# Two wide chunks in the second up unit of each group, and the moved block read a unit sooner

## The reference

```python
h = rmsnorm(x, norm_mlp[l])
x = x + jnp.square(jax.nn.relu(h @ w_up[l])) @ w_down[l]
```

## Time and profile before

| | |
|---|---|
| median of 3 runs | 2680.71 us |
| span of the profiled execution | 2676.6 us |
| TensorE products busy | 2663.6 us (100%) |
| DVE busy | 2049.1 us (77%) |
| ACT busy | 1447.3 us (54%) |
| wide chunks (L1336) | 166 |
| plain chunks of 1024 (L1315) | 762 |

### The profile page before, as it was taken

The page is one execution under the profiler, slowest core; times in us unless marked ns, Lnnn a source line. Parts: engine busy times, 40 slices in busy tenths (PEclk is TensorE's granted clock), DMA queues, the critical chain, the costliest instruction groups (busy, mean ns, idle before and its releaser), DMA issues.

```text
span 2676.6 us, 37287 instructions
## 1 busy us (share of the span) xinstructions
PE 2663.6 (100%) x13592; PEld 2234.4 (83%) x13592; DVE 2049.1 (77%) x3019; ACT 1447.3 (54%) x1863; POOL 128.0 (5%) x220
## 2 busy tenths in 40 slices
PE   9999999999999999999999999999999999999998
PEld 7788778888888888888887887788888888888887
DVE  5665568977798897987756655689678988989875
ACT  5545555545665555655455455555456556556554
POOL 0100000000100100100010000000001001000000
PEclk9999999999999999999999999999999999999999
DMA  7875545676775766766687655466677767667574
GB/s 259 234 238 165 181 158 183 227 243 234 233 232 192 242 220 205 241 208 225 233 231 230 215 169 178 157 201 229 227 258 236 227 201 241 211 218 231 191 247 151
DMA packets 179960, 575.55 MB, mean 215 GB/s; under 512 B 23016, under 2 KB 43028, under 8 KB 179664
## 3 DMA queue, kind: packets, MB, share of 16 engines
q1 hardware_dynamic: 166256, 536.94, 61.4%
q0 software_dynamic: 13008, 35.98, 5.1%
q10 hardware_dynamic: 528, 0.37, 0.1%
HBM read 535.15 MB, written 38.04 MB: 214 GB/s over the span
## 4 chain that ended last, share of the span: by engine, by line
PE 98%; DVE 1%; DMA 0%; issue 0%; ACT 0%; POOLq 0%; POOL 0%; ACTq 0%
PE acc L530 25%; PE acc L532 25%; PE acc L531 25%; PE att L500 2%; PE att L498 2%; PE att L499 2%; PE acc L498 2%; PE acc L500 2%; PE acc L499 2%; PE acc L548 1%; PE acc L547 1%; PE acc L546 1%; PE turn L499 1%; PE turn L500 1%; PE turn L498 1%; PE att L625 0%
## 5 line engine op out<-in xcount | busy, mean ns | idle before, releaser
L1315 DVE TENSOR_TENSOR w_lo<-raw,w_hi 128x1024 fp32r<-128x1024 f32 (+1 forms) x778 | 935.2, 1212 | 422.8 <-ACT w_hi L890 420.1
L890 ACT ACTIVATE w_hi<-raw 128x1024 fp32r<-128x1024 f32 (+1 forms) x778 | 813.7, 1052 | 683.9 <-PE acc L532 512.6
L530 PE MATMUL acc<-w_hi,h_hl 128*128 128x512 f32 x1848 | 736.7, 399 | 1.0 <-DVE w_lo L1315 0.9
L532 PE MATMUL acc<-w_hi,h_hl 128*128 128x512 f32 x1848 | 729.0, 394 | 0.0
L531 PE MATMUL acc<-w_lo,h_hl 128*128 128x512 f32 x1848 | 728.5, 394 | 0.0
L530 PEld LDWEIGHTS acc<-w_hi,h_hl 128*128 128x128 f32 x1848 | 347.9, 188 | 84.1 <-issue 5.5
L532 PEld LDWEIGHTS acc<-w_hi,h_hl 128*128 128x128 f32 x1848 | 347.8, 188 | 81.5
L531 PEld LDWEIGHTS acc<-w_lo,h_hl 128*128 128x128 f32 x1848 | 348.3, 188 | 75.9
L1336 DVE TENSOR_TENSOR w_lo<-raw,w_hi 128x1792 fp32r<-128x1792 f32 x166 | 335.5, 2021 | 41.2 <-ACT w_hi L899 40.2
L530 PE MATMUL acc<-w_hi,o_hl 128*128 128x512 f32 x912 | 361.0, 396 | 0.0
L531 PE MATMUL acc<-w_lo,o_hl 128*128 128x512 f32 x912 | 359.9, 395 | 0.0
(11 more groups left out here) (297 smaller groups left out, 3493.6 us busy)
## 6 DMA issues: line engine op xcount, KB each, us to landing
raw<-in_w_main SPq DMA_DIRECT2D x928, 512.0 KB, 4.2
scratch<-spread SPq DMA_DIRECT2D x37, 512.0 KB, 2.8
moved<-scratch SPq DMA_DIRECT2D x148, 128.0 KB, 3.4
scratch<-spread POOLq DMA_DIRECT2D x30, 512.0 KB, 3.4
moved<-scratch POOLq DMA_DIRECT2D x120, 128.0 KB, 5.1
raw<-in_w_misc SPq DMA_DIRECT2D x16, 336.0 KB, 4.7
bias_b<-bias_rows POOLq DMA_DIRECT2D x32, 96.0 KB, 5.2
xs<-in_x SPq DMA_DIRECT2D x4, 512.0 KB, 7.2
```

Of the source, the lines that this page charges most:

```text
L530: nc.tensor.matmul(o, a_hi, hi[:, kk], start=(k == 0), stop=False)
L532: last = nc.tensor.matmul(o, a_lo, hi[:, kk], start=False, stop=fin)
L890: nc.scalar.activation(w_hi[s][:, 0:2 * width], raw[r][:, 0:2 * width], ACT.Copy).then_inc(hi_ready, 1)
L1315: nc.vector.tensor_tensor(w_lo[s][:, 0:2 * width], raw[r][:, 0:2 * width], w_hi[s][:, 0:2 * width].bitcast(F32), ALU.subtract).then_inc(lo ...
```

## The change

U72 and U8, the second up unit of each group, are computed with two wide chunks of eight: chunks 1 and 3 in U72, chunks 5 and 7 in U8 (`WIDE_FIRST`). Their sides go to the banks att2 and turn (`SIDES_OF_UP`). So `take_up` of this unit becomes `take_side`, `add_up_sides` and `take_summed` in U16. The group's first moved block (`u_moved(g, 0)`) is read after chunk 7 of U8 or U72 instead of chunk 2 of U16, and its sums are split after chunks 0 and 1 of U16 instead of chunk 7. The transposition `spread_u(g, 1)` stands after chunk 6 of U16 instead of chunk 4. In the last group the sums are formed as well, and `take_summed` stands ahead of chunk 4.

```diff
-WIDE_UP = ((1, 3, 5), (), (1, 3, 5, 7), ())
+WIDE_UP = ((1, 3, 5), (1, 3), (1, 3, 5, 7), ())
+WIDE_FIRST = (5, 7)
+SIDES_OF_UP = (0, 1, 0)
```

On TensorE:

```diff
-                up(C_MLP + 8, 1, adds(0, 0), 1)
+                up(C_MLP + 8, 1, adds(0, 0), 1, [(c, h_sums_took, (G_SUMS + H_SUMS) * l + G_SUMS + c // 2 + 1) for c in WIDE_FIRST],
+                   WIDE_FIRST)
...
-                    up(g * 64 + (C_MLP + 72), 1, adds(g, 3), 1)
+                    up(g * 64 + (C_MLP + 72), 1, adds(g, 3), 1, wide=WIDE_UP[1])
```

On ACT, U8, U16, U72 and last U16:

```diff
-                run(C_MLP + 8, {3: lambda: take_up(0, 0, base + 8, 0)}, {1: lambda: h_sums(3)})
+                run(C_MLP + 8, {3: lambda: take_up(0, 0, base + 8, 0)}, {1: lambda: h_sums(3), 7: lambda: u_moved(0, 0)},
+                    WIDE_FIRST, steps_at(0, -len(WIDE_FIRST)))
...
-                    run(g * 64 + (C_MLP + 16), {5: lambda: take_up(g, 1, end + 16, 1)},
-                        {2: lambda: u_moved(g, 0), 7: lambda: u_sums_hi(g, 0)}, WIDE_UP[2], steps_at(g, AT_UP2))
+                    run(g * 64 + (C_MLP + 16), {3: lambda: take_side(g, 1, end + 16), 6: lambda: take_summed(g, 1, sides_count(g, 0))},
+                        {0: lambda: u_sums_hi(g, 0)}, WIDE_UP[2], steps_at(g, AT_UP2))
...
-                    run(g * 64 + (C_MLP + 72))
+                    run(g * 64 + (C_MLP + 72), (), {7: lambda: u_moved(g, 4)}, WIDE_UP[1], steps_at(g, AT_UP1))
...
-                run(C_MLP + 64 * g + 16, {3: lambda: take_up(g, 1, end + 16, 1)}, {2: lambda: u_moved(g, 0)},
-                    WIDE_UP[2], steps_at(g, AT_UP2))
+                run(C_MLP + 64 * g + 16, {3: lambda: take_side(g, 1, end + 16), 4: lambda: take_summed(g, 1, sides_count(g, 0))},
+                    {0: lambda: u_sums_hi(g, 0)}, WIDE_UP[2], steps_at(g, AT_UP2))
```

On DVE, the same four:

```diff
-                run(C_MLP + 8, {2: factors}, {1: lambda: h_sums(3), 3: lambda: spread_u(0, 0)})
+                run(C_MLP + 8, {2: factors}, {1: lambda: h_sums(3), 3: lambda: spread_u(0, 0), 7: lambda: u_moved(0, 0)},
+                    WIDE_FIRST, steps_at(0, -len(WIDE_FIRST)))
...
-                        {2: lambda: u_moved(g, 0), 4: lambda: spread_u(g, 1), 7: lambda: u_sums_lo(g, 0)}, WIDE_UP[2], steps_at(g, AT_UP2))
+                        {1: lambda: u_sums_lo(g, 0), 3: lambda: add_up_sides(g, 1, NBLK), 6: lambda: spread_u(g, 1)},
+                        WIDE_UP[2], steps_at(g, AT_UP2))
...
-                    run(g * 64 + (C_MLP + 72), (), {5: lambda: take_down(g, 3, end + 72)})
+                    run(g * 64 + (C_MLP + 72), (), {5: lambda: take_down(g, 3, end + 72), 7: lambda: u_moved(g, 4)},
+                        WIDE_UP[1], steps_at(g, AT_UP1))
...
-                run(C_MLP + 64 * g + 16, (), {2: lambda: u_moved(g, 0, False), 3: lambda: spread_u(g, 1)},
+                run(C_MLP + 64 * g + 16, (), {1: lambda: u_sums_lo(g, 0), 3: lambda: add_up_sides(g, 1, NBLK), 4: lambda: spread_u(g, 1)},
                     WIDE_UP[2], steps_at(g, AT_UP2))
```

## The result

| | time, us (median, range) | ratio to before | span of the profiled execution |
|---|---|---|---|
| before | 2680.87 (2679.57 to 2681.46) | | 2676.6 |
| changed | 2709.27 (2707.53 to 2714.64) | 1.0112 [1.0100, 1.0124] | 2707.5 |

What follows compares the result with a forecast made beforehand. The prediction took TensorE, 98% of the chain, to bound the kernel as long as weight splits arrive in time. Its terms, -5.1 + 5.7 + 4.2 + 6.0 + 6.6 = +17.4, gave 2698.1 us, range 2686 to 2704.

Steps and rivals of the forecast that it cites:

- The saving: U8 and U72: two wide chunks in each of eight units save 0.32 us apiece, 5.1 us in all.
- Term 2, the early block: First U16 of each layer: TensorE waits for block 0's landing; with chunk 4's wait 5.7 and 4.2 us.
- Nothing of the change moves that spread: U8: block 0 is still spread at 673.5 in layer 0, so it lands at 688.0; layer 1's landing stays 2013.9.
- rival (d): First U16: TensorE's clock falls in the landing wait, losing 2 us, twice; +21, 2702 us; chance 0.09.
- the 1.9 at chunk 4: U16: DVE needs 12.55 us for TensorE's 10.64, so without lead TensorE waits 1.9 us at chunk 4.
- Term 3, DVE's way back: Loop's four returns: an instruction refetch delays DVE, so TensorE waits 1.5 us at each, 6.0 us in all.
- Term 4, behind the loop: Last U16 and last U24: the earlier take costs 2.0, block 1's later landing 1.3 a layer; 6.6 us together.
- The step that failed: Loop's U24: the block lands 8 us later but DVE's work fits, so it costs nothing.
- (a): Whole kernel: the waits are hidden and the gain stands, 2675.6 us; chance 0.08.
- (b): Whole kernel: every cost comes except the refetch at the loop's returns, +11.4, 2692.1 us; chance 0.15.
- (c): Whole kernel: only block 0's wait costs, +4.8, 2685.5 us, not told from no change; chance 0.08.

Runs made afterwards that it cites:

- e4: The changed kernel with 14 unused products added on TensorE ahead of each layer's first U16, filling the landing wait: 2712.1 us, ratio 1.0114.
- e2: The changed kernel without the wide chunks in U8 and U72, block 0 still read a unit sooner, block 1 spread in chunk 4 again: 2691.1 us, ratio 1.0047.
- e10: e3 with block 0 spread ahead of chunk 3's split in U8, and the last group's take at chunk 6, block 1's steps later too: 2690.6 us.
- e3: The changed kernel padded with 105 tiny DVE memsets, so that the loop's DVE instructions touch three blocks of 128 instead of four: 2703.4 us, ratio 1.0085.
- e6: The kernel before with 70 tiny DVE memsets in layer 1, so that its loop touches four instruction blocks instead of three: 2679.8 us, ratio 0.9999.
- e7: e3 with the summed unit taken and block 1 spread one chunk sooner in the loop's U16: 2704.1 us, ratio 1.0097.
- e9: The changed kernel, not padded, with block 0 spread ahead of chunk 3's split in U8 instead of behind it: 2702.9 us, ratio 1.0089.

## Why the prediction was right or wrong

**The saving** held: U72 0.60 us shorter six times, U8 0.49 and 0.50, 4.6 instead of 5.1.

**Term 2, the early block**, had the right mechanism and landing: ACT read block 0 at 688.46 (688.0 forecast) and TensorE waited 3.81 us (3.8). Two things failed. The step "Nothing of the change moves that spread" did not hold in layer 1: block 0 left 14.3 us ahead of U8's end instead of 16.1, its read came 1.4 us ahead of that end instead of the 3.65 that follow from my 2013.9 and 2017.55, and the split of chunk 0 ended 4.54 behind it instead of 2.3. In layer 0 the wait came out in part by luck: the block left 15.2 us ahead of U8's end, where it had been 16.5, and took 13.3 us to the read, where I had reckoned with 13.9. And rival (d), at 0.09, came true in both layers: the clock at 0.50 for 6.83 us, of which TensorE worked for 6.05 and 5.13 us, so some 3.0 and 2.6 us lost, where I had reckoned 2 each. In exchange the 1.9 at chunk 4 did not appear. e4 shows that these two stand in for each other. The Trainium skill ("TensorE: Matmul & The Clock Gate", Part 1) says that idleness re-throttles, and e4's full clock agrees; how long a wait brings a dip these runs do not tell: in e2 the wait of 3.15 us had one and that of 3.22 had none, in e10 2.04 had one and 2.03 had none.

**Term 3, DVE's way back**, was right in kind and size: idle for 3.0 to 3.5 us at all four returns, waits of 1.73, 1.61, 1.98 and 1.41 at chunk 4 for a forecast of 1.5 each. e3 removes it by alignment alone, e6 shows that it was hidden before. The Trainium skill ("Runtime: NRT & Kernel Launch", Instruction fetch mechanics) says that a taken branch outside the window stalls; e3 has the same branches and no stall, so the stall depends on how many blocks of 128 instructions the body touches, four or three. The size of 16 KiB that the page gives is that of the packets of q8, TensorE's (107 packets, 1.75 MB), and not of q14's, which have 8 KB. Blocks of 256 instructions, of which two are held, would not explain DVE's stalls either: in the changed kernel layer 1's loop begins 1383 DVE instructions behind layer 0's, and with these at most one of the two would stall; both did.

**Term 4, behind the loop**: 1.83 a layer in the last U16 for a forecast of 2.0, by the mechanism named. Last U24 took -0.34 and +0.72 where I had added 1.3 each: mis-sized by 2.2 us in all, which hid a part of what the sum left out.

**The step that failed** is the sentence at the end of term 4, "In the loop's U24 the block also lands 8 us later, but U24 has no wide chunk and its DVE work fits: nothing". I had counted DVE's work in U24 and found room, but not asked who waits for the landing, nor what blocks 2 and 3 and the weights do when all leave later with a ring that U16 has already drained, nor that D40 adds sides of its own and needs the lead that is then gone. It cost 10.5 us where the sum has nothing; e2, without the wide chunks and the late block 1, has 1.2 there, and e7, with block 1 leaving a chunk sooner, 3.3. Together with the clock and layer 1's landing that is why 17.4 became 30.8 us of span.

Rivals (a), (b) and (c) fell. (a) would have needed a landing before 684; e9, which brings it forward, still pays 5.0 in the first U16s through chunk 4.

## What to carry to other kernels

Moving a step that hands a buffer on moves everything behind that hand-over: follow the landing, the next block and the weights one unit further than the unit that is edited. Work that two engines hand to and fro (here ACT, DVE, ACT, DVE for the sides) stalls both rings, and how many chunks of lead it needs can be sized from a place in the kernel that already does it, as last U24 gave last U16's price here. Before a wait is costed by a clock dip or a slip of another engine, ask what catches up during it; and where a loop's body nears a whole number of instruction blocks, its start matters as much as its length.

## What the runs showed of the hardware

- Behind the return of a loop body of 339 to 360 DVE instructions, DVE stood idle for 2.5 to 3.5 us where the body touches four blocks of 128 instructions (8 KB packets on q14), and for 0.3 or less where it touches three. 105 memsets of a single element, elsewhere, took that away.
- The dips of the granted clock inside the kernel lasted 3.41 or 6.83 us, nothing else. They began within waits of TensorE or up to 1.5 us behind them, the waits being of 2.0 to 4.5 us; waits of 2.0, 2.8 and 3.2 us passed without one.
- Of a block of 512 KB that goes to memory and back, the time from the spread to the read that waited for it was 11.0 to 14.1 us (block 0 in the changed kernel, e4 and e9, counted from the second of the two transpositions). What makes the difference was not tested.
